# State space tile pieces placed one at a time between the first block's softmaxes, and norm sums of both addends in the same PSUM columns

## The reference, cut to what matters

```
# first block, attention: three dilated windows, combined by their log-sum-exp
sc = einsum(q, k) * scale + alibi bias, masked;  p = exp(sc - m);  o = p v / den
# first block, state space branch: a complex diagonal recurrence over 512 steps
x[t] = (ab_re + i ab_im) * x[t-1] + bu[t];  y = Re(c x) + d_skip * u
# every norm
rmsnorm(x, g) = x * rsqrt(mean(x * x, axis=-1) + 1e-6) * g
# second block: x = x + 0.5 * rmsnorm(f, g1), and the next sublayer starts with rmsnorm(x, g2)
```

## Time and profile before

| | us |
|---|---|
| median of three runs | 2537.99 |
| lowest and highest of them | 2535.80, 2540.66 |
| the profiled execution, its own time | 2535.33 |
| span of the profile, first to last instruction | 2533.5 |

### The profile page before, as it was taken

How to read it: one execution, slowest core, us unless ns; L and a number is a source line. 1 busy time by engine, 2 the same in 40 slices (tenths; PEclk the granted TensorE clock), 3 DMA queues, 4 the chain that set the end, 5 groups by cost and what they waited for, 6 DMA issues and landing times.

```text
span 2533.5 us, 32662 instructions
## 1 busy us (share of the span) xinstructions
PE 2485.5 (98%) x11304; PEld 1987.3 (78%) x11304; DVE 1329.0 (52%) x1844; ACT 908.6 (36%) x1294; POOL 972.3 (38%) x384
## 2 busy tenths in 40 slices
PE   6999999999999999999999999999999999999998
PEld 3777778888788887777788888788887778788886
DVE  8856677256431348667531348430348667531344
ACT  3444543234431234553431233321334554431331
POOL 1332324443344443233344443344443333344443
PEclk8999999999999999999999999999999999999998
DMA  5221553322233231222133232233231222132232
GB/s 232 90 73 64 203 200 124 116 92 91 74 101 107 96 105 64 84 83 100 63 101 110 94 110 71 75 107 103 97 107 60 86 87 94 66 106 89 95 104 79
DMA packets 69702, 253.37 MB, mean 100 GB/s; under 512 B 8928, under 2 KB 11104, under 8 KB 68480
## 3 DMA queue, kind: packets, MB, share of 16 engines
q1 hardware_dynamic: 69632, 252.46, 29.7%
HBM read 244.76 MB, written 2.10 MB: 97 GB/s over the span
## 4 chain that ended last, share of the span: by engine, by line
PE 85%; issue 11%; POOL 2%; DVE 2%; ACT 0%; POOLq 0%; DMA 0%; SPq 0%; DVEq 0%; ACTq 0%
PE unit_bank L509 26%; PE unit_bank L510 26%; PE unit_bank L511 26%; PE score L596 3%; POOL w_lo L471 2%; PE mix L652 1%; PE out_bank L632 1%; PE mix L551 1%; PE score L901 1%; PE out_bank L557 1%; PE mix L660 0%; DVE x L1875 0%; DVE unit_bank L1873 0%; PE stat_bank L565 0%; PE score L652 0%
## 5 line engine op out<-in xcount | busy, mean ns | idle before, releaser
L471 POOL TENSOR_TENSOR w_lo<-raw,w_hi 128x1024 fp32r<-128x1024 f32 (+2 forms) x376 | 967.1, 2572 | 1539.6 <-ACT w_hi L949 1539.6
L509 PE MATMUL unit_bank<-u_hi,w_hi 128*128 128x512 f32 x2160 | 849.8, 393 | 4.3 <-POOL w_lo L471 4.3
L949 ACT ACTIVATE w_hi<-raw 128x1024 fp32r<-128x1024 f32 (+2 forms) x376 | 416.9, 1109 | 1194.0 <-PE unit_bank L511 1169.5
L510 PE MATMUL unit_bank<-u_lo,w_hi 128*128 128x512 f32 x2160 | 841.4, 390 | 0.0
L511 PE MATMUL unit_bank<-u_hi,w_lo 128*128 128x512 f32 x2160 | 841.4, 390 | 0.0
L509 PEld LDWEIGHTS unit_bank<-u_hi,w_hi 128*128 128x128 f32 x2160 | 405.8, 188 | 106.7 <-issue 16.0
L511 PEld LDWEIGHTS unit_bank<-u_hi,w_lo 128*128 128x128 f32 x2160 | 405.8, 188 | 85.4
L510 PEld LDWEIGHTS unit_bank<-u_lo,w_hi 128*128 128x128 f32 x2160 | 406.0, 188 | 84.4 <-issue 1.9
L509 PE MATMUL unit_bank<-h_hi,w_hi 128*128 128x512 f32 x992 | 387.0, 390 | 0.2 <-DVE h_lo L1745 0.2
L511 PE MATMUL unit_bank<-h_hi,w_lo 128*128 128x512 f32 x992 | 385.9, 389 | 0.0
L510 PE MATMUL unit_bank<-h_lo,w_hi 128*128 128x512 f32 x992 | 385.9, 389 | 0.0
(11 more groups left out here) (316 smaller groups left out, 1947.3 us busy)
## 6 DMA issues: line engine op xcount, KB each, us to landing
raw<-in_w_gate_up SPq DMA_DIRECT2D x168, 512.0 KB, 3.4
raw<-in_w_down SPq DMA_DIRECT2D x64, 704.0 KB, 4.1
raw<-in_w_in SPq DMA_DIRECT2D x66, 512.0 KB, 3.5
raw<-in_w_up SPq DMA_DIRECT2D x30, 512.0 KB, 3.4
f<-in_w_ada_rows SPq DMA_DIRECT2D x26, 512.0 KB, 4.9
raw<-in_w_out SPq DMA_DIRECT2D x24, 512.0 KB, 3.5
raw<-in_w_down SPq DMA_DIRECT2D x16, 512.0 KB, 3.5
ada_in_u<-in_w_ada SPq DMA_DIRECT2D x4, 1024.0 KB, 10.7
```

The costliest lines, as they stand in the source:

```text
L471: e.tensor_tensor(w_lo[:, s, 0:n], raw[:, s, 0:n], as32(w_hi[:, s, 0:n]), ALU.subtract).then_inc(lo_ready, 1)
L509: e.matmul(bank[:], wh, hi(k), start=n == 0, stop=False)
L510: e.matmul(bank[:], wh, lo(k), start=False, stop=False)
L949: e.activation(w_hi[:, s, 0:n], raw[:, s, 0:n], ACT.Copy).then_inc(hi_ready, 1)
```

## The change

Pieces of the state space work: `scanned` is cut in two (`scanned`, the two scans, and `turned_back`, the products behind them), and the pieces go elsewhere. `turned` now first waits until the tile before has been turned back. `outputs` on TensorE, and the copies of its results on ScalarE, go one unit earlier.

```diff
                 def turned():
+                    if j:
+                        e.wait_ge(scan_ready, j)
                     double(CHUNKS // 2, 2 * j, 2, p1, p2)
...
                     step(e.tensor_tensor_scan(bi, r, p5, 0.0, ALU.mult, ALU.add))
+
+                def turned_back():
                     e.tensor_tensor(p1, c_t, br, ALU.mult)
...
-                    if n < 4:
-                        tiles[n // 2]()
-                    elif j == 0:
+                    if n == 2 and j < 3:
+                        (tiles[0].scanned, tiles[1].turned_back, tiles[3].turned)[j]()
+                    if n >= 4 and j == 0:
                         grow(C_grown, STRIDE + 1, per_state("c_re"), per_state("c_im"), True, (n // 2 - 2,), (4, 6))
                         if n == 6:
                             e.sem_inc(C_ready, 1)
+                            tiles[0].turned_back()
+                            tiles[1].turned()
+                            tiles[1].scanned()
+                    if n == 6 and j == 1:
+                        tiles[2].turned()
+                        tiles[2].scanned()
+                        tiles[2].turned_back()
+                    if n == 6 and j == 2:
+                        tiles[3].scanned()
+                        tiles[3].turned_back()
+            tiles = [scan_parts(j) for j in range(HEAD_PAIRS)]
+            tiles[0].turned()
             for j in range(HEAD_PAIRS):
                 heads(j)
```

```diff
-                    if j == HEAD_PAIRS - 1 and n:
-                        outputs(n - 1)
+                    if j == HEAD_PAIRS - 1 and n < 2:
+                        outputs(n)
...
-                    if last and n >= 2:
-                        e.wait_ge(y_done, n - 1)
+                    if last and n in (1, 2):
+                        e.wait_ge(y_done, n)
```

```diff
-            def token_sums(bank, at, src, apart=1):
+            def token_sums(sums, src, first=True, last=True):
                 for b in range(TB):
-                    n = at + apart * b
-                    mm = e.matmul(bank[:, n:n + 1], src[:, b * P:(b + 1) * P], tab("ones", 0, 1), start=True,
-                                  stop=True)
+                    mm = e.matmul(sums[:, b:b + 1], src[:, b * P:(b + 1) * P], tab("ones", 0, 1),
+                                  start=first and b == 0, stop=last and b == TB - 1)
...
-                token_sums(out_bank, 0, f_acc, 2)
+                token_sums(square_sum, f_acc, last=False)
...
-                token_sums(out_bank, 1, f_sq, 2).then_inc(sums_ready, 1)
+                token_sums(square_sum, f_sq, first=False).then_inc(sums_ready, 1)
...
-                keep_warm(6)
+                keep_warm(3)
...
-                e.wait_ge(sums_ready, r + 1)
-                e.tensor_reduce(f_sum, out_bank[:, 0:2 * TB].rearrange("p (b n) -> p b n", n=2),
-                                mybir.AxisListType.X, ALU.add).then_inc(f_summed, 1)
...
-                        step(e.tensor_tensor(grown, gf_sum, inv_f, ALU.mult))
+                        step(e.tensor_tensor(scaled, gf_sum, inv_f, ALU.mult))
                         if r:
-                            step(e.scalar_tensor_tensor(grown, cross_sum, 2.0, grown, ALU.mult, ALU.add))
+                            step(e.scalar_tensor_tensor(grown, cross_sum, 2.0, scaled, ALU.mult, ALU.add))
                             step(e.tensor_tensor(grown, grown, inv_f, ALU.mult))
-                            step(e.tensor_tensor(x_sum, x_sum, grown, ALU.add))
+                            e.wait_ge(grown_ready, r)
+                            e.tensor_tensor(x_sum, x_sum, grown, ALU.add).then_inc(grown_ready, 1)
...
-                        e.tensor_copy(grown, x_sum).then_inc(grown_ready, 1)
```

The norm behind the products into x gets the same sums (its reduce goes too), and in VectorE's loop over the chunks the square of chunk k is added in turn k instead of k+1; the last square stays with TensorE:

```diff
-                if k:
-                    e.wait_ge(sq_ready, k)
-                    step(e.tensor_tensor(x_acc if k == DC - 1 else stat_bank[:], stat_bank[:], sq[:, (k - 1) % 2, :],
+                if k < DC - 1:
+                    e.wait_ge(sq_ready, k + 1)
+                    step(e.tensor_tensor(x_acc if k == DC - 2 else stat_bank[:], stat_bank[:], sq[:, k % 2, :],
                                          ALU.add))
                     e.sem_inc(sq_used, 1)
```

More of the change, by code:

```diff
@@ L15 @@
+from collections import namedtuple
 from contextlib import ExitStack
@@ L152, in program @@
         f_sq, gf_sq, f_acc, cross, cross_acc, gf_acc = (slot(n) for n in range(6))
-        f_sum, root_f, root_u, inv_f, inv_u, grown = (slot(11)[:, 128 + 4 * n:132 + 4 * n] for n in range(6))
+        root_f, root_u, inv_f, inv_u, scaled = (slot(11)[:, 128 + 4 * n:132 + 4 * n] for n in range(5))
         x_sum = stat[:, 0:TB]
@@ L202, in program @@
         unit_bank, stat_bank, score, mix, out_bank = banks[0:2], banks[2], banks[3:5], banks[5:7], banks[7]
+        square_sum, gf_sum, cross_sum, grown = out_bank[:, 0:TB], mix[0][:, 0:TB], mix[0][:, TB:2 * TB], mix[0][:, 2 * TB:3 * TB]
         z_bank = banks[3:7]
@@ L214, in program @@
         u_full, u1_full = sem("u_full"), sem("u1_full")
[L215 to L218, removed]
+        x1_sums, x1_root, x1_inverse, x1_spread = (
+            sem(n) for n in ("x1_sums", "x1_root", "x1_inverse", "x1_spread"))
+        sums_ready, cross_ready, cross_sums, grown_ready, root_ready, inverse_ready, spread_ready, rstd_ready = (
+            sem(n) for n in ("sums_ready", "cross_ready", "cross_sums", "grown_ready", "root_ready",
                              "inverse_ready", "spread_ready", "rstd_ready"))
@@ L585, in norm @@
                 e.wait_ge(cross_ready, r + 1)
-                mm = token_sums(mix[0], 0, gf_acc)
+                mm = token_sums(gf_sum, gf_acc)
                 if r:
-                    mm = token_sums(mix[0], TB, cross_acc)
+                    mm = token_sums(cross_sum, cross_acc)
                 mm.then_inc(cross_sums, 1)
-                keep_warm(6)
+                keep_warm(3)
                 for s in range(2):
@@ L882, in _ @@
             e.wait_ge(sq_used, 1 + DC - 1)
-            token_sums(out_bank, 0, x_acc, 2)
+            token_sums(square_sum, x_acc, last=False)
             keep_warm(3)
             e.wait_ge(sq_ready, DC)
-            token_sums(out_bank, 1, sq[:, 1, :], 2).then_inc(x1_sums, 1)
+            token_sums(square_sum, sq[:, 1, :], first=False).then_inc(x1_sums, 1)
             keep_warm(1)
@@ L983, in norm @@
                 f_squares(p, 1, part, DC - 1, g)
-                e.wait_ge(f_summed, r + 1)
-                token_root(root_f, f_sum)
+                e.wait_ge(sums_ready, r + 1)
+                token_root(root_f, square_sum)
                 if not ahead:
@@ L997, in norm @@
                         e.wait_ge(grown_ready, r + 1)
-                        token_root(root_u, grown)
+                        token_root(root_u, x_sum)
                 e.wait_ge(spread_ready, 2 * r + 2)
@@ L1165, in _ @@
             squares_along(0, OUT1, DC - 1)
-            e.wait_ge(x1_summed, 1)
-            e.activation(root_f, f_sum, ACT.Sqrt, bias=eps[:], scale=1.0 / D).then_inc(x1_root, 1)
+            e.wait_ge(x1_sums, 1)
+            e.activation(root_f, square_sum, ACT.Sqrt, bias=eps[:], scale=1.0 / D).then_inc(x1_root, 1)
             e.wait_ge(mod_ready, 2)
@@ L1556, in _ @@
             e.wait_ge(bu_ready, 4)
+            Tile = namedtuple("Tile", ("turned", "scanned", "turned_back"))
             def scan_parts(j):
@@ L1582, in scanned @@
                     e.tensor_tensor(bi, p3, p4, ALU.add).then_inc(scan_ready, 1)
-                return turned, scanned
+                return Tile(turned, scanned, turned_back)
             def split_out(j):
@@ L1617, in take_probs @@
                         pT_ready, 1)
-                tiles = scan_parts(j)
                 for h in range(2):
@@ L1699, in gated_update @@
                         take_update(p0 + i, s, 2 * i + s, gate)
-            e.wait_ge(x1_sums, 1)
-            e.tensor_reduce(f_sum, out_bank[:, 0:2 * TB].rearrange("p (b n) -> p b n", n=2),
-                            mybir.AxisListType.X, ALU.add).then_inc(x1_summed, 1)
             e.wait_ge(x1_root, 1)
@@ L1823, in norm @@
                         e.wait_ge(cross_sums, r + 1)
-                        gf_sum, cross_sum = mix[0][:, 0:TB], mix[0][:, TB:2 * TB]
-                        step(e.tensor_tensor(grown, gf_sum, inv_f, ALU.mult))
+                        step(e.tensor_tensor(scaled, gf_sum, inv_f, ALU.mult))
                         if r:
-                            step(e.scalar_tensor_tensor(grown, cross_sum, 2.0, grown, ALU.mult, ALU.add))
+                            step(e.scalar_tensor_tensor(grown, cross_sum, 2.0, scaled, ALU.mult, ALU.add))
                             step(e.tensor_tensor(grown, grown, inv_f, ALU.mult))
-                            step(e.tensor_tensor(x_sum, x_sum, grown, ALU.add))
-                        else:
-                            step(e.tensor_tensor(x_sum, grown, inv_f, ALU.mult))
```

(5 more changed lines are left out.)

2 lines of the change are left out of this document (1 added, 1 removed).

## The result

The changed kernel takes 2546.24 us (median of 7 runs, 2542.3 to 2547.8); the kernel before, beside it, 2534.99 (7 runs, 2533.53 to 2540.66). The ratio is 1.0038, 95% interval 1.0029 to 1.0047: slower, by 11 us between the medians and 9.6 by the ratio. The forecast was 2544.6 in a range of 2536.5 to 2551, with 0.63 for slower.

A forecast was written before the change was run, and what follows sets the result against it. PE was taken to bound the kernel, busy 98% of the span. Pieces +4.0, products into x +8.8 and norms -6.2 gave +6.6 on 2535.33, 2541.9; plus 2.7 for the median, 2544.6, range 2536.5 to 2551.

The forecast's parts named there:

- Pieces, gains: Head pairs: moved pieces end PE's waits at the transposes and `outputs`; -3.1 and +0.1 in pair 0, -1.3 in pairs 2 and 3.
- The pile ahead of `turn_v`: Pairs 0 to 1: VectorE work behind n = 6, plus GpSimd splits, takes 21.3 us against 14.37, making `turn_v` late: +7.0.
- rival that VectorE keeps GpSimd out: Pairs 0 to 1: gapless SBUF products hold GpSimd's splits back, `turn_v` only 1.2 late, 2534.4 us; chance 0.11.
- The products into x: Loop into x: VectorE waits for squares behind ScalarE's refill; +1.4 in units, +4.9 at the tail, sum +8.8 with tile and clock.
- The tile: Last refill into x: its weight tile, behind delayed `w_ada` loads on SyncE, comes late: +2.0, ends 0 and +3.
- The clock: Behind PE's idle ahead of `turn_v` and ahead of the row sums, lower granted clock costs +1.6 and +1.2.
- "clock and loads" rival: Both waits and the tile: each idle costs two low clock stretches, tile 3 us late, three whole splits: 2549.3; chance 0.13.
- The norms: All norms: no reduce, fewer `keep_warm`, `grown` in PSUM; gains sum to -6.2, ends -3 and -8.
- r = 3: Norm 3: earlier root and first products, and no late fifth chunk: -1.2; norms 1 and 4 alike.
- r = 2: Norm 2: cross terms come last and no chunk was late, so 0.2 + 0.7 = 0.9 gained.
- `grown` in PSUM: Norms: the four-column product at line 1828 falls from 1.75 us to about 0.16, removing the fifth chunk's lateness.
- `keep_warm`: Ahead of the norms' first products: three matmuls less save 0.7 us.

The follow-up runs named there:

- Experiment 9: The changed kernel with `turned` 1 and `scanned` 1 moved from behind block 6 of pair 0 to behind blocks 0 and 2 of pair 1: 2538.03 us, ratio 1.0005.
- Experiment 6: The changed kernel with ScalarE's square of chunk k put ahead of the refill that waits for unit k+1: 2533.58 us, ratio 0.9986.
- experiment 5: The changed kernel with 27 unused identity matmuls ahead of `turn_v` between pairs 0 and 1 and 29 ahead of the row sums: 2539.12 us, ratio 1.0009.
- experiment 1: The kernel before with only the new placement of the state space pieces, `outputs` and the copies of their results: 2539.47 us, ratio 1.0013.
- experiment 2: The kernel before with only the changed loop of products into x, adding the square of chunk k behind update k: 2550.29 us, ratio 1.0053.
- experiment 3: The kernel before with only the changed norms: `grown` in PSUM, no reduces, three `keep_warm` less: 2527.95 us, ratio 0.9963.
- experiment 4: The changed kernel with 48 unused identity matmuls ahead of `turn_v` between pairs 0 and 1 and 52 ahead of the row sums: 2547.13 us, ratio 1.0043.
- experiment 7: The kernel before with the changed norms, its own loop into x, and the pieces placed anew across the pairs: 2519.45 us, ratio 0.9931.
- experiment 8: The kernel before with only the changed norms, but `grown` kept in SBUF: 2531.40 us, ratio 0.9982.
- experiment 10: The kernel before with only the changed norms, but six `keep_warm` matmuls ahead of the first products, not three: 2530.24 us, ratio 0.9977.

## Why the prediction was right, and where not

**Pieces, gains.** Right: -3.0 in pair 0, -1.3 in pairs 2 and 3 each, against -2.5, -1.7 and -1.5. The 0.9 us of waits at line 808 are the ones that I had left in pair 2.

**The pile ahead of `turn_v`.** Right in mechanism and size: 7.0 forecast, 6.47 seen, VectorE the releaser. The blocking that I put at 5.8 us for three splits reads from the three long instructions: 2.50 against 1.67 for two of `grow`, 2.60 and 2.80 against 0.42 and 0.67, so 0.8 + 2.2 + 2.1 = 5.1. The rival that VectorE keeps GpSimd out is refuted by the same rows: GpSimd came in at all three splits, at two of them in a gapless run of SBUF products. Experiment 9 takes two pieces away and the wait goes.

**The products into x.** The mechanism was right: VectorE stands until ScalarE has refilled and squared. Experiment 6 shows it by changing ScalarE's order alone. Two sizes were short. Up to unit 6 two units waited as forecast; unit 2 to unit 6 takes 23.66 us for 21.92, so they cost 1.7 and not 1.4 (the other 0.2 of the table is a longer wait for GpSimd ahead of unit 2). Unit 7 waited too, 0.56 us, which lies in the tail and which I had left out. The tile was late by 2.8 and not 2.0 (ScalarE wants it 0.2 behind the end of unit 6, which was at 351.9): SyncE's queue after had this,

```profile
345.45 0.80 SPq L384 DMA_DIRECT2D f<-in_w_ada_rows  x2
346.30 0.91 SPq L405 DMA_DIRECT2D arena<-in_w_up  x2
347.34 2.99 SPq L324 DMA_DIRECT2D raw<-in_w_up  x2
```

where before it was

```profile
334.33 0.80 SPq L382 DMA_DIRECT2D f<-in_w_ada_rows  x2
...
338.05 5.77 SPq L322 DMA_DIRECT2D raw<-in_w_up  x2
```

The start (345.45) is about the 340.4 forecast and the 4.6 us of the pieces, but six tiles and not five were issued within 5 us. That the sixth made the tile late is an argument from the queue; no run leaves it out. The last refill started at 354.96, as ScalarE's timeline after shows, with the square behind it:

```profile
354.96 1.06 ACT L950 ACTIVATE w_hi<-raw 128x1024 fp32r<-128x1024 f32 x1 [6.94 <-DMA raw<-in_w_up]
355.92 0.61 ACT L956 ACTIVATE arena<-x 128x512 f32<-128x512 f32 x1
```

**The clock.** This is the term that was off most. I priced what an idle PE loses behind the two waits at 1.6 and 1.2, from one wait of 2.9 us and the unit behind it. By the fillers of experiment 5 it was 2.9 (9.59 to 6.68) and 5.1 (12.54 to 7.47). Behind waits of 6.5 and 7.1 us the stretch at 1.2 GHz was longer, as two windows after show (the clock is the third number from the end):

```profile
128.00:138.20 10.20, 6.38 (x19) 4.86 (x20) 5.53 (x16) 1.49 (x4) 0.87 (x1) 0.50 0.13 51
363.50:377.20 13.70, 11.96 (x55) 10.29 (x56) 4.02 (x9) 1.80 (x4) 0.00 (x0) 0.50 0.50 191
```

Both begin while PE still waits. For the sums I had even set an end at 1.7, though their 60 short matmuls lie inside the low stretch almost to the last. The "clock and loads" rival had this cause and I gave it only 0.5 us more for the sums. Of the 5.9 us by which the profile exceeds my sum of +6.6, 1.3 + 3.9 are here by the two fillers' windows.

The same wait is not always followed by as much of it. In experiment 6 the pile and its wait of 6.46 us are unchanged, but the low stretch is this one:

```profile
129.70:136.50 6.80, 3.90 (x13) 2.96 (x14) 4.54 (x16) 0.99 (x3) 0.00 (x0) 0.50 0.22 77
```

There the work behind it lost 1.8 us (8.39 for 6.62), close to my 1.6. Experiment 9, with 6.9 us of waiting ahead of the sums, has 0.50 for the 17.0 us from 350.3 on. So 2.9 and 5.1 belong to the profiled execution, and what sets the length of the stretch stays open.

**The norms.** The total is right (-6.1 for -6.2), and so is r = 3 (-1.19 for -1.2), but the total is in part luck: from r = 0 to r = 5 the norms gained 0.54, 2.25, -0.75, 1.19, 1.19 and 0.87. In r = 1 the kernel before was at 1.2 GHz from 1001.3 to 1004.7 and the changed kernel was not, which gave 1.06 that I had not counted; r = 2 took it away again. The gain in r = 1 is hardly chance of one execution: with the norms of before (before, experiments 1 and 2) r = 1, 3 and 4 take 22.48 us five times and 23.53 four times, and with those of the change (after, experiments 3 to 7 and 9) 21.28 or 21.29 in all 21. Why the low stretch stays away there is not shown. The split of the forecast was not right either: experiments 8 and 10 give 0.75 to `grown` in PSUM and 0.35 to the three `keep_warm`, which leaves 0.1 for the reduce and the copy; I had started from 0.7 for `keep_warm`. r = 2 took 25.50 us, 0.75 more than before, where I had -0.9: its stretch at half clock was 6.8 us and not 3.4 in this execution, and in experiment 3, where it was 3.4, it takes 23.86. The last norm gained 0.8 for 0.2, with 1.7 us less at half clock.

The Trainium skill ("VectorE: DVE Perf Modes", section "The TRN2 errata") would make each of the two instructions on `grown` dearer from PSUM. The trace disagrees. Two groups after that read `grown` from PSUM:

```profile
L1839 DVE TENSOR_TENSOR mix<-mix,arena 128x4 f32<-128x4 f32 x5 | 0.9, 171 | 0.2
L1841 DVE TENSOR_TENSOR stat<-stat,mix 128x4 f32<-128x4 f32 x5 | 0.8, 158 | 0.2
```

The second of them before, when it read `grown` from SBUF, behind the end of the split:

```profile
L1829 DVE TENSOR_TENSOR stat<-stat,arena 128x4 f32<-128x4 f32 x5 | 0.8, 163 | 0.2
```

158 ns against 163 for the same sum: nothing is added. The Trainium skill ("SBUF — State Buffer", section "Who interferes with whom") has the rule that a VectorE instruction with at most one input in SBUF, outside the modes that use both ports, does not contend with GpSimd. The trace agrees: 171 ns against 1746 in experiment 8, for nothing but the place of `grown`.

**The number.** 2544.6 for 2546.24 is closer than the sum deserves, and that is luck. I added 2.7 us for the distance from the profiled execution to the median of three runs; in the seven runs beside the changed kernel the median of before was 2534.99, so there was no distance. The difference measured is +11.2 between the medians and +9.6 by the ratio, and the sum said +6.6.

## What to carry to other kernels

Count an engine's queue from one deadline to the next, with what other engines block in it, before work is moved. That 17.4 us of work would not fit in the 16.2 us up to the deadline, even before GpSimd's splits, could be read off the profile, and the same count gave the placement of experiment 7, some 8 us faster than that of before. When a consumer is moved one iteration closer to its producer, look at what stands ahead of the producer in its own queue: here a refill that waits for the next unit. Price an idle TensorE by the work that comes behind it too: here 60 small matmuls at half clock cost 5.1 us behind a wait of 7.1. If a wait of this length can't be removed, matmuls that compute nothing and end just before the wait does can give that part back, as in experiment 5.

## What the runs showed of the hardware

- Idle of 6.5 and 7.1 us of PE came with 10.2 and 13.7 us at 1.2 GHz in the changed kernel; with the idle filled up to 0.45 and 0.99 us, with none. In experiments 6 and 9 idle of 6.5 and 6.9 us came with 6.8 and 17.0.
- A four-column product with both operands in SBUF takes 1.75 us beside a split of GpSimd, 0.17 with one of them in PSUM. A product of 256 columns takes 2.60 for 0.42 (experiments 8 and 3; after): the cost is what is left of the other engine's instruction, not the size of one's own.
- A scan (two SBUF operands) stands still in the same way: 2.80 us for 0.67.
